# A decoder layer with experts on one core: G block by half tiles, the sample tile's output projection in the score banks, transposed router logits, and a reordered routing with dummy matmuls

## What is computed

```python
def layer(p, lam_init, x, ...):
    z = rmsnorm(x, p['norm_mix_g']) @ p['w_in']
    gq, gk, gv, gr, ga, pu, dq, dk, dv = split(z)
    mix = concat(gated_linear_attention, window_means, differential_attention)
    x = x + mix @ p['w_out']
    x = x + memory_attend(rmsnorm(x, p['norm_mem_g']), mk, mv, p['w_mem_q'], p['w_mem_o'])
    x = x + hier_moe(rmsnorm(x, p['norm_ffn_g']), ...)   # best of 4 groups, best 2 of its 4 experts
```

## Time and profile before

| | us |
|---|---|
| median of 3 runs | 733.04 (732.08 to 735.81) |
| profiled execution | 732.52 |
| its span, first to last instruction | 730.6 |
| TensorE busy in it | 676.3 (93%) |
| VectorE busy | 522.6 (72%) |
| ScalarE busy | 425.0 (58%) |
| granted TensorE clock, mean | 0.973 |

### The profile page before, as it was taken

One profiled execution on the slowest core, in us unless ns is written; L12 is line 12 of the kernel. 1 busy time (PEld: TensorE's weight loads), 2 busy tenths in 40 slices (PEclk: granted clock), 3 DMA queues, 4 the chain that ended last, 5 costly groups with the idle time before them and its releaser, 6 DMA issues.

```text
span 730.6 us, 9430 instructions
## 1 busy us (share of the span) xinstructions
PE 676.3 (93%) x3469; PEld 544.4 (75%) x3469; DVE 522.6 (72%) x697; ACT 425.0 (58%) x602; POOL 142.1 (19%) x160
## 2 busy tenths in 40 slices
PE   4999999998999999889999499999999999999991
PEld 3898887776666776778888278888888888888861
DVE  4436655565877674656457778899999999988883
ACT  6646643244664443454233358887777788888880
POOL 4102850011001011000001302222222122222134
PEclk9999999999999999999999579999999999999996
DMA  8623232403771000310094869999999999999863
GB/s 307 220 74 148 113 146 78 155 0 131 266 299 69 1 1 31 125 46 1 1 359 150 343 242 359 369 382 366 383 374 375 383 369 375 382 371 386 307 218 121
DMA packets 32867, 161.23 MB, mean 221 GB/s; under 512 B 6189, under 2 KB 6523, under 8 KB 18108
## 3 DMA queue, kind: packets, MB, share of 16 engines
q1 hardware_dynamic: 23392, 140.39, 50.3%
q0 software_dynamic: 5344, 10.27, 5.2%
q10 hardware_dynamic: 4092, 10.08, 3.8%
HBM read 149.59 MB, written 20.03 MB: 232 GB/s over the span
## 4 chain that ended last, share of the span: by engine, by line
PE 75%; DVE 12%; DMA 5%; issue 2%; ACT 2%; POOL 1%; SPq 1%; ACTq 0%; POOLq 0%; DVEq 0%
PE pj L2110 43%; PE scores L2110 14%; PE tr_v L2110 10%; DVE wl L1412 4%; PE tr_a L2118 2%; PE scores L2490 2%; PE tr_v L2118 2%; DMA acc_rows<-y,idx_sb 1%; DMA xs_next<-acc_rows,idx_sb 1%; PE tr_a L2519 1%; DMA xT_raw<-in_xT 1%; DVE w_lo L1441 1%; DVE hid L1412 1%; DMA xg<-h_rows,idx_sb 1%; POOL rs L749 1%
## 5 line engine op out<-in xcount | busy, mean ns | idle before, releaser
L1412 DVE TENSOR_TENSOR wl<-moe_raw,wh 128x2048 fp32r<-128x2048 f32 x96 | 218.5, 2290 | 28.2 <-ACT wh L901 26.2
L901 ACT ACTIVATE wh<-moe_raw 128x2048 fp32r<-128x2048 f32 x96 | 182.3, 1919 | 37.8 <-PE pj L2110 12.6
L2110 PE MATMUL pj<-w_hi,xT_hi 128*128 128x512 f32 (+2 forms) x192 | 70.7, 368 | 9.1 <-DVE w_lo L1441 8.3
L747 POOL TENSOR_SCALAR rs<-stat 128x1 f32<-128x1 f32 (+4 forms) x31 | 10.7, 344 | 320.6 <-DVE stat L1623 158.6
L2110 PE MATMUL pj<-w_hi,xT_lo 128*128 128x512 f32 (+2 forms) x192 | 68.9, 359 | 0.0
L2110 PE MATMUL pj<-w_lo,xT_hi 128*128 128x512 f32 (+2 forms) x192 | 68.8, 358 | 0.0
L802 POOL DMA_INDIRECT acc_rows<-y,idx_sb x14 | 22.3, 1591 | 207.7 <-ACT y L1335 193.6
L2110 PE MATMUL pj<-wh,xgh 128*128 128x512 f32 x128 | 52.8, 412 | 1.4 <-DVE xgl L1412 1.4
L1441 DVE SCALAR_TENSOR_TENSOR w_lo<-raw,pack_a,w_hi 128x512 fp32r<-128x512 f32 (+2 forms) x64 | 43.8, 745 | 11.8 <-ACT w_hi L945 11.8
L2110 PE MATMUL tr_v<-wh,xgh 128*128 128x512 f32 x128 | 51.1, 400 | 0.0
L2110 PE MATMUL pj<-wh,xgl 128*128 128x512 f32 x128 | 51.0, 398 | 0.0
(11 more groups left out here) (416 smaller groups left out, 1483.5 us busy)
## 6 DMA issues: line engine op xcount, KB each, us to landing
moe_raw<-in_w_exp_gate SPq DMA_DIRECT2D x32, 1024.0 KB, 8.4
moe_raw<-in_w_exp_up SPq DMA_DIRECT2D x32, 1024.0 KB, 9.9
moe_raw<-in_w_exp_down SPq DMA_DIRECT2D x32, 1024.0 KB, 10.0
raw<-in_dense SPq DMA_DIRECT2D x16, 1024.0 KB, 6.0
raw<-in_dense SPq DMA_DIRECT2D x8, 256.0 KB, 6.4
x_rows<-in_x_prompt SPq DMA_DIRECT2D x4, 512.0 KB, 11.6
xw<-in_x_prompt ACTq DMA_DIRECT2D x1, 2048.0 KB, 8.4
h_rows<-h ACTq DMA_DIRECT2D x4, 512.0 KB, 3.8
```

Source lines behind the costliest of these rows:

```text
L747: link(pool.tensor_scalar(rs[rows, n, cs], stat[rows, n, cs], EPS, None, ALU.add))
L901: act.activation(wh[s4][:, :], moe_raw[n % RING][:, :], ACT.Copy).then_inc(hi_done, 1)
L1412: return dve.tensor_tensor(out, a, b, op)
L2110: return pe.matmul(out, lhsT, rhs, start=start, stop=stop, skip_group_check=True)
```

## The change

1. **Start.** x tiles 0, 1 and 2 are loaded, rounded and subtracted by halves of 512 columns, tile 1's first half between the third and fourth quarter of the first weight unit. G runs part 0 of tiles 0 and 1, then part 1 of both, part 0 and 1 of tile 2, then tiles 3 and 4, in four banks. The constants come in two transfers, the 27 columns first. Row loads and their squares come later.
2. **First join.** The sample tile's projection goes to two score banks (4 and 5 of `pj_of`), in halves around `x1_T(0)` and `mixd_T`; its additions move behind `q_T(0)` and `max_m(0)`; the rounding of the second memory output unit and the square of tile 4 move behind the first exponentials.
3. **Router** of tiles 2 to 4: stationary router weights, transposed result in a score bank, copied by ScalarE, transposed back. `moe_input(3)` and `moe_input(4)` run before the last two logits.
4. **Routing**: groups and experts in one search; `pos` by 11 matmuls; both lists of `placed` in one product, one reduction, two comparisons; the list of tokens ahead of the gate values; gate tables and `gates` behind expert 0's first matmuls; 17, 6 and 22 dummy matmuls; units 6 and 7 wait for the first gather.

```diff
 def projection_plan():
-    plan = [((b, t), row_reader(t)) for b, _, _ in IN_BLOCKS[:-1] for t in range(TILES)] + ...
+    plan = [(("G", t), row_reader(t), (0, 1, 2, 3, 0)[t]) for t in range(TILES)]
...
-    plan += [(("w_out", c, TILES - 1), "V", 1 - c) for c in range(2)]
-    plan += [(("mem_q", 0), "A")]
+    plan += [(("w_out", c, TILES - 1), "V", 4 + c) for c in range(2)]
+    plan += [(("mem_q", 0), "A", 1)]
...
+        pj_more = [sc[:, 1024:1536], sc[:, 1536:2048], sc[:, 0:512], sc[:, 512:1024]]
+        pj_of = lambda key: (pj + pj_more)[PJ[key][3]]
@@ sync
+            for g in range(2):
+                x_half(0, g)
+                for k in range(4):
+                    quarter(g, k)
+                    if (g, k) == (0, 2):
+                        x_half(1, 0)
+            x_half(1, 1)
+            x_half(2, 0)
+            x_half(2, 1)
+            x_load(3)
+            rows_load(0)
+            rows_load(1)
+            x_load(4)
+            rows_load(2)
             dense_load(2)
...
                     elif n < RING:
+                        sp.wait_ge(xg_in[0], 16)
                         sp.wait_ge(acc_out, 16 * TILES)
@@ gpsimd
-            pool.wait_ge(chosen_ready, 1)
+            pj_read(pool, ("w_mem_o", 1, TILES - 1))
             pool.memset(xg[:, :, :], 0.0).then_inc(xg_clear, 1)
-            pool.memset(xs[:, :], 0.0).then_inc(xg_clear, 1)
...
             gather(1, idx_sb[:, 1:2])
+            pool.memset(xs[:, :], 0.0).then_inc(xg_clear, 1)
@@ scalar
-            act.dma_start(pack_a[:, :], A["pack_a"]).then_inc(gains_in, 16)
+            act.dma_start(pack_a[:, 0:27], A["pack_a"][:, 0:27]).then_inc(gains_in, 16)
...
+            x1_high(0, (1,))
             mixd_high(TILES - 1)
-            x1_high(0)
+            x1_high(0, (0,))
...
             mq_out(0)
-            x1_square(TILES - 1)
             w_high(MO_UNIT)
-            w_high(MO_UNIT + 1)
...
             exps_m(0)
+            w_high(MO_UNIT + 1)
+            x1_square(TILES - 1)
...
             x2_square(TILES - 1)
+            logits_out(2)
+            x2_out(TILES - 1)
             h3_out_of(TILES - 2)
-            x2_out(TILES - 1)
+            logits_out(3)
+            logits_out(4)
             h3_out_of(TILES - 1)
@@ vector
+            x1_T(0, (1,))
             mixd_low(TILES - 1)
-            x1_T(0)
+            x1_T(0, (0,))
             w_low(MQ_UNIT)
-            add_rows("w_out", 0, TILES - 1, xw, xw)
             w_low(MQ_UNIT + 1)
             x1_T(1)
-            add_rows("w_out", 1, TILES - 1, xw, xw)
...
             q_T(0)
+            add_rows("w_out", 0, TILES - 1, xw, xw)
             max_m(0)
+            add_rows("w_out", 1, TILES - 1, xw, xw)
             w_low(MO_UNIT)
...
             x2_T(TILES - 2)
+            x2_T(TILES - 1)
             logits(2)
             moe_input(TILES - 2)
-            x2_T(TILES - 1)
+            moe_input(TILES - 1)
             logits(3)
-            moe_input(TILES - 1)
             logits(4)
...
+            first_best(lg[:, :, :].rearrange("p t (g i) -> p t g i", g=5), in_fives(m5), in_fives(k5), all5, rank_5)
...
+            tt(r160.rearrange("p (i n) -> p i n", i=2), both, at_pos, ALU.mult).then_inc(pj_dve, 1)
+            link(dve.tensor_reduce(scratch[:, 2740:2750], r160.rearrange("p (n e) -> p n e", e=E), AX.X, ALU.add))
+            for i in range(2):
+                tt(placed[:, i], lane[:, :].unsqueeze(1).to_broadcast([P, TILES, P]), bc(posi[i], P), ALU.is_equal)\
+                    .then_inc(place_ready, 1)
...
             x_lo(0, 0)
+            gates_held()
             for j in range(3):
                 split_lo(0, 0, j)
+                if j == 1:
+                    gates_out()
@@ tensor
-            in_block("G", 2, {})
+            for part in range(2):
+                for t in range(2):
+                    pe.wait_ge(xT_lo_done, 2 * part + t + 1)
+                    project(("G", t), t, *x_block(t), BLOCK_UNITS["G"], WIDTH["G"], part)
...
+            x1_T(0, (1,))
+            sc_read(pe, ("diff", 4, HEADS - 1, 0))
+            w_out(0, TILES - 1, 0)
             mixd_T(TILES - 1)
-            x1_T(0)
-            w_out(0, TILES - 1, 0)
+            w_out(1, TILES - 1, 0)
+            x1_T(0, (0,))
             w_out(0, TILES - 1, 1)
-            w_out(1, TILES - 1)
+            w_out(1, TILES - 1, 1)
             x1_T(1)
...
+            def router_T(t):
+                sc_read(pe, ("mem", TILES - 1))
+                for g in range(2):
+                    tr_read(pe, ("x2", t, g))
+                out = sc[0:20, 512 * (t - 2):512 * (t - 2) + ROWS[t]]
+                for k in range(KB):
+                    ins = mm(out, wr[:, k, :], hT[:, t % 2, k, 0:ROWS[t]], k == 0, k == KB - 1)
+                ins.then_inc(sc_full, 1)
...
             x2_T(TILES - 2)
-            router(2)
+            router_T(2)
             x2_T(TILES - 1)
-            router(3)
-            router(4)
+            logits_T(2)
+            router_T(3)
+            router_T(4)
+            logits_T(3)
+            logits_T(4)
+            keep_warm(17)
             pe.wait_ge(chosen_ready, 1)
...
+            keep_warm(6)
             j = claim("pj", PJ, PJ_KEYS, ("entries",), pj_act, pj_dve)
...
-            keep_warm(6)
-            pe.wait_ge(gheld_ready, 1)
...
-            keep_warm(4)
+            keep_warm(22)
...
             x_turn(0, 0, 16)
-            pe.wait_ge(xl_done, 2)
-            pj_read(pe, ("gates",))
+            pj_read(pe, ("entries",))
             for part in range(2):
+                pe.wait_ge(xl_done, part + 1)
                 gate_or_up(pg[0], 0, part, part, part + 1)
+            gates()
```

More of the change, by code:

```diff
@@ L141, in high_plan @@
     plan += [("mix_g", TILES - 1)] + [("mix_d", t) for t in range(TILES - 1)]
[L142 removed]
+    plan += [("x1", 0, 1), ("mix_d", TILES - 1), ("x1", 0, 0)] + [("x1", 1, g) for g in range(2)]
     for t in range(TILES):
@@ L154, in score_plan @@
     plan += [(("mem", t), "A") for t in range(TILES)]
+    plan += [(("lt", t), "A") for t in range(2, TILES)]
     return plan
@@ L1492, in _ @@
             link(dve.memset(lg[:, :, :], 0.0))
-            for n in range(2):
-                x0_low(n)
-                w_low(n)
-            for t in range(1, TILES):
-                x_low(t)
+            x_half_low(0, 0, 1)
+            w_low(0)
+            x_half_low(1, 0, 2)
+            x_half_low(0, 1, 3)
+            w_low(1)
+            x_half_low(1, 1, 4)
+            for g in range(2):
+                x_half_low(2, g, 5 + g)
+            x_low(3)
+            x_low(4)
             for t in range(TILES):
-                if t in (2, 3):
-                    w_low(t)
-                if t == 4:
+                if t in (1, 2):
+                    w_low(t + 1)
+                if t == 3:
                     n = ROW_AT[("G", 4)]
@@ L1758, in _, with x1_T @@
                     add_rows("w_out", 1, t - 1, xw, xw)
-            def x1_T(t):
-                for g in range(2) if t else (1, 0):
+            def x1_T(t, gs=(0, 1)):
+                for g in gs:
                     ks = slice(4 * g, 4 * g + 4)
@@ L1906, in _ @@
[L1906 to L1918 removed]
+            group, group_max, best = all5[:, :, 0, :], in_fives(m5)[:, :, 0], in_fives(m5)[:, :, 1:5]
@@ new lines, in _ @@
+            first_best(lg[:, :, :].rearrange("p t (g i) -> p t g i", g=5), in_fives(m5), in_fives(k5), all5, rank_5)
+            link(dve.scalar_tensor_tensor(out=by_group(r80[0]), in0=all5[:, :, 1:5, :], scalar=-1e30, in1=ev,
+                                          op0=ALU.mult, op1=ALU.add))
+            tt(hot1, all5[:, :, 1:5, :], bc(group, 4), ALU.mult)
+            first_best(by_group(r80[0]), r20[3], r20[4], hot2, rank_g)
+            link(tt(hot2, hot2, bc(group, 4), ALU.mult))
+            tt(chosen[:, :, :], r80[1], r80[2], ALU.add).then_inc(chosen_ready, 1)
@@ new lines, in _ @@
+            for i in range(2):
+                ins = tt(held[:, i], r80[i + 1].unsqueeze(2).to_broadcast([P, TILES, 2, E]), bc(entry[:, :, :], E), ALU.mult)
+            link(ins)
+            dve.wait_ge(pj_full, PJ[("pos",)][0] + 1)
+            both = scratch[:, 340:500].rearrange("p (i n) -> p i n", i=2)
+            at_pos = pj[PJ[("pos",)][3]][:, 0:80].unsqueeze(1).to_broadcast([P, 2, 80])
+            tt(r160.rearrange("p (i n) -> p i n", i=2), both, at_pos, ALU.mult).then_inc(pj_dve, 1)
@@ L2553, in step @@
                     next_share(1)
+                if first:
+                    pj_read(pe, ("gates",))
                 for c in range(2):
```

210 lines of the change are left out of this document (112 added, 98 removed).

## The result

The changed kernel takes 721.85 us (median of 4, 720.05 to 724.6) where the kernel before took 732.56 beside it: a ratio of 0.9851, 95% interval 0.9804 to 0.9898. A second set gave 722.06 us (median of 6) and 0.9860 [0.9834, 0.9887]. The forecast was 721.0 in 717 to 727.

The account below looks back on a forecast made before the run. The prediction took TensorE's work, plus the places where it waits or runs at low clock, to bound the kernel. Savings of 1.2, 3.6 and 7.0 us, together 11.8, gave 720.7 and with the median's half microsecond 721.0 us, range 717 to 727.

Parts of the forecast that it names:

- Part A: Start: G by halves, x tile 1's first half sent earlier and constants in two pieces save 1.2 us, bounds 0 and 1.6.
- That fills the idle 0.87 us: Start: G by halves over tiles 0 and 1 fills TensorE's 0.87 us wait for x tile 1.
- I take 0.3: Start: sending the constants in two pieces takes 162 KB out of the way, 0.4 us at full rate, counted as 0.3.
- Part B: First join of difference and memory attention: reordered projection and moved additions save 3.6 us, bounds 1.5 and 4.4.
- -4.4: First join: the memory query starts at 301.7 instead of 306.14 us, 4.4 us sooner.
- TensorE to wait 0.8 us there: First memory tile: weight split ahead of the first softmax's normalisation and rounding ahead of tile 1's evacuation cost TensorE 0.8 us.
- Part C: Routing join: earlier gate start 5.7 and warm gate 3.0, less 1.7 for VectorE's lateness, save 7.0 us, bounds 3 and 8.
- (1): Routing join: transposed router tile takes the same 1.8 us, copies and transposes back add 0.3; logits complete at 401.45 us.
- estimate of 3.2 us for 512 KB: First gather: 2.0 us plus bytes over 436 GB/s gives 3.2 us, rows at 413.6; the forecast took 4.4 instead.
- The sum: Whole kernel: the start, first join and routing join together save 11.8 us, 720.7 on 732.52; with the median's half microsecond, 721.0.
- Transfers set the pace: Rival, expert stage: the weight stream limits the end, units 6 and on start later, 736.5 us; chance 0.03.

Follow-up runs that it names:

- a_alone: Only the start's change (G by halves, x in halves, constants split) put into the kernel before; 729.21 us, ratio 0.9953.
- c_alone: Only the routing join's change put into the kernel before; 727.15 us, ratio 0.9913.
- before: The kernel before the change, first profile, no edit; profiled execution 732.52 us.
- b_alone: Only the first join's change (sample tile's output projection in the score banks, halves around the transposes) put into the kernel before; 729.95 us, ratio 0.9953.
- no_dummies: The changed kernel without its 17, 6 and 22 dummy matmuls in the routing; 724.54 us, ratio 0.9874 to the kernel before.
- order: The changed kernel with the low half of the first w_mem_o unit split moved behind the first normalisation, in two pieces; 720.49 us, ratio 0.9830 to the kernel before.
- order_plain: The changed kernel with the first w_mem_o unit's low half behind the first normalisation and the router's products in their old form; 723.93 us, ratio 0.9877.
- no_list_dummies: The changed kernel without the 22 dummy matmuls behind the entries, the 17 and 6 kept; 723.44 us, ratio 0.9873 to the kernel before.
- after: The changed kernel with the whole change, first set and profile; 721.85 us, ratio 0.9851 to the kernel before.
- after_again: The changed kernel run once more without an edit, for a second profile; 722.06 us, ratio 0.9860 to the kernel before.

## Why the prediction was right, point by point

**Part A, predicted -1.2, bounds 0 and -1.6: too small by two.** The mechanism is as told, halves of G fill the stretches without work. The size was that of one execution. Four profiles with the old start have K at 167.7 to 170.2 (the last with the clock low at 18 to 22 us), mean 168.7; ten with the new one at 165.9 to 166.8, mean 166.4: 2.4 us, and 3.4 by the runs of a_alone [2.1, 4.8]. The term that was mis-sized is "That fills the idle 0.87 us": with the wait for G's second unit it is 2.0 to 2.4 us in the three other executions. The term for the constants, "I take 0.3", is seen nowhere: the first matmul begins at 7.41 to 8.27 us in the four profiles with the old start and at 7.40 to 8.36 in the ten with the new one. The gap alone, 1.9 us on the mean of the four, and a low clock in one of them (c_alone, 1.8 us at 18 to 22) make up the 2.4. The last 1 us between 2.4 and 3.4 isn't explained; 2.4 lies inside the interval of the runs.

**Part B, predicted -3.6.** The step "-4.4" for the query's start, from a row with a low clock, was 4.7 us (Q-K 138.44 to 133.7); against the two executions without that fall it is 3.1 to 3.2. That fall, at 294 to 302 us, is in two of the four profiles with the old join (before and c_alone) and in none of the ten with the new one. The step "TensorE to wait 0.8 us there" was 1.1 (M-Q 80.06 to 81.18), from the split that it named. What it lacked is that the clock may fall at other places: at 175 to 180 us for 1.5 us (135.3 for 133.7), and at 308 to 316 for 1.3 (82.5 for 81.2). Over its seven runs b_alone gives -3.4, where the sum said -3.6.

**Part C, predicted -7.0: X-M fell from 62.30 to 55.23, -7.1.** By its steps, counted from M: routing starts 0.4 later (predicted 0.3); the choice takes 4.0 us for 4.9, as said; the list stands 2.8 sooner (2.9); the gather lands in 4.41 us (4.4); the gate starts 5.4 sooner (5.7) and takes 5.72 us (5.5); what follows, until expert 2's transposes, gives back 1.2 for the 1.7 taken, by 26.06 - 24.46 = 1.6 gained less the gate's own 2.8. The runs give 6.4 [5.3, 7.4].

One step was right in size and wrong in sense. (1) booked the transposed router as a cost of 0.3 us, "as neither is shown to be free". The 0.3 to 0.4 is there, and yet without the new form X-M is 2.0 to 2.7 us longer: only with it did the 17 dummies begin at full clock. The rows of the kernel before gave no warning under the routers themselves (clock 1.00); the low clock at 402 us stands in idle time.

The Trainium skill, TensorE: Matmul & The Clock Gate, "What's actually happening", was cited for a clock that is throttled unless activity lifts it. The runs agree as to the two levels (0.50 and 1.00 in the windows of no_dummies and of order), and show one stretch that its words would not lead one to expect: 6.00 of 6 us busy, clock 0.50. The estimate of 3.2 us for 512 KB, worked out from the Trainium skill, DMA: Bandwidth & Descriptors, "Anatomy of one DMA", no gather here came near: the first one took 4.41 us alone on the queues.

**The sum.** -11.8 predicted. (732.52 - 11.8 plus the half microsecond of the median is 721.2; the forecast says 721.0.) By the parts' own runs -3.4, -3.4 and -6.4, together -13.2; by the whole -10.3 [-8.3, -12.2] in the same set. So the forecast was close in part by luck, because errors cancel: A was too small by 2, and part of that is lost again in what the sum did not have. The falls at the two new places cost 2.8 us where they come, some 1.5 on the mean if five of nine is their rate; the rest of the 2.9 between the parts and the whole is inside the intervals. *Transfers set the pace* is refuted: SyncE's wait for VectorE's splits was 243.0 us and is 227.1, and an expert still takes 17.98 us (expert 2's, 3's and 4's rows are transposed at 439.80, 457.78 and 475.76). SyncE's waits in the changed kernel, 380 to 720 us (total, times, longest):

```profile
SPq L627 <- DVE wl L1448: 227.1, 87, 4.3
...
SPq L627 <- DMA xg<-h_rows,idx_sb: 7.0, 1, 7.0
```

The new wait costs SyncE 7.0 us once, and no engine is seen to wait for what it holds back.

## What to carry to other kernels

Read a gap that ends with a transfer or a clock at its low level in more than one execution before it becomes a term: here one was less than half of what the other executions showed, and one was a fall of the clock that the next profile did not have. When a small transfer on which everything waits meets bulk loads, hold the loads behind its landing: without that the gather took nearly twice as long, and all of the routing join's gain hung on it. And read the granted clock under the last real work, in more than one execution, before adding dummies behind it: where it had fallen, 17 dummies took up to 6.8 us for 4.2 and held up the work they were to help.

## What the runs showed of the hardware that was not expected

TensorE's clock can fall in the midst of work without a gap. In order_plain it was full until 395.5 us, 0.64 in the half microsecond after and 0.50 from 396, during 32 router products of 20 moving columns that began at 394.99 and took 4.87 us. In order 32 of 128 columns ran at 1.00 (2.82 us), but so did the 32 of 20 columns in the four profiles with the old routing join (3.00 us).

How soon the clock falls in idle time depended on what ran before. Behind the 32 products of 20 columns it fell after 0.4 to 0.6 us, in each of those four. In no_dummies, behind the transposed form, TensorE is idle from 399.51 and the clock full until 401.9. In no_list_dummies, behind 23 dummies and the list's products, it is idle from 403.65 and the clock full until 407.9. The last two are one profile each, and which property of the work decides isn't shown.

The same program has the fall at 175 to 180 us in some executions and not in others. Of the nine profiles that have both the new start and the new join, five have it, with K at 166.40 to 166.76, and four do not, with K at 165.90 to 166.39. The work around is the same, a wait of 1.00 us for plT_lo at 176 us included; the five have the later starts, if only by 0.01 us at the border, and lose 1.5 us. In four of the five the clock falls again at 308 to 316 us (in no_dummies at 320 to 324), in none of the four others. Yet b_alone has the fall at 311 to 315 without the one at 175 (Q-K 133.88, M-Q 82.39), so the second doesn't need the first. Whether the start decides wasn't tried. In the last column two things are open: end-X is 0.8 us more in three of the profiles (after, after_again, c_alone) and 2.1 more in order_plain, with the same code at the end. The experts are as long there (17.98 us from one to the next); the difference arises behind the transposes of the last one's rows.
